# Two successive norms folded into one scale at the second mixer's entry

## The chip, the cores and the metric

One core of one Trainium2 chip runs the whole program. The time is the device time of one execution, in microseconds; of several executions the median is given. The engines are TensorE (PE, with its weight loads as PEld), VectorE (DVE), ScalarE (ACT), GpSimd (POOL) and SyncE (SP), which here issues nearly all DMAs. Each engine works its own queue in order and waits on semaphores that the others raise.

## The reference

Two transformer blocks follow one another on one sequence of 256 tokens with 1024 features, in float32. The place of the change is the seam between them: the first block ends in a norm, and the second begins with another one, with a modulation worked out from a vector `c`.

```python
def rmsnorm(x, w, eps=NORM_EPS):
    xf = x.astype(jnp.float32)
    y = xf * lax.rsqrt(jnp.mean(xf * xf, axis=-1, keepdims=True) + eps)
    return (y * w.astype(jnp.float32)).astype(x.dtype)

# first_block, end
    h = h + 0.5 * swiglu_ffn(rmsnorm(h, ffn2_norm[layer]), ffn2_w_in[layer], ffn2_w_out[layer])
    return rmsnorm(h, final_norm)

# second_block
    mod = c_act @ w_ada[l] + b_ada[l]
    shift1, scale1, gate1, shift2, scale2, gate2 = [m[:, None, :] for m in jnp.split(mod, 6, axis=-1)]
    h = rms_norm(x, g_pre_mix[l]) * (1.0 + scale1) + shift1
    y = token_mixer(h, cos, sin, w_in[l], conv_w[l], conv_b[l], ...)
    x = x + gate1 * rms_norm(y, g_post_mix[l])

# token_mixer, beginning
    z = h @ w_in
    u_glu, q_lat, kv_lat, k_r, gate_logits = jnp.split(z, IN_SPLIT, axis=-1)
    ua, ub = jnp.split(u_glu, 2, axis=-1)
    u = ua * jax.nn.sigmoid(ub)
    u = causal_depthwise_conv_2(u, conv_w, conv_b)
    u = jax.nn.silu(layer_norm(u, conv_norm_g, conv_norm_b))
```

The convolution has 31 taps on 1024 channels. The gains of the final norm are a vector, so the second norm's sum of squares is that of the first norm's output with the gains in it.

## The kernel before

Activations lie transposed, features on the 128 partitions and tokens along the row: `resid` holds eight tiles of 128 x 256. Each matrix product takes one slab of weights at a time (`PLAN` lists all 153), 128 x 2048 numbers, 256 output columns wide. A slab is loaded by SyncE into one of three slots (`raw`), ScalarE casts it to its high part (`wh`, `cast`), VectorE subtracts to get the low part (`wl`, `sub`), and TensorE makes three products for each weight tile: high by high, high by low, low by high (`wide`, line 1681). A slot's load waits for the subtraction of the slab three before, its cast for that slab's products (`taken`). The activations are split the same way into `xh` and `xl`. There is no scheduler: the order on each engine is the order in which its function is written.

The feed-forward part of the first block (`ffn`) ends with a slab whose product fills four banks; behind it VectorE adds bank after bank to the residual (line 1153, `ffn2_resid` counts 4). Then, before:

- GpSimd squares the residual pair by pair (`squares`, line 568) into `kn`, ScalarE squares it with the final norm's gain (line 874) into `qn`, and TensorE sums both over the features by products with a matrix of ones (`column_sums`, line 1709).
- VectorE multiplies the residual by the gain in place (line 1385), makes the modulation vectors `ada` and `mods` (lines 1389 to 1399), takes the first root's reciprocal `rstd` (line 1095), forms the second mean from both sums (lines 1403, 1405), waits for ScalarE's second root (line 877), takes its reciprocal, and scales tile by tile (line 1412). ScalarE adds the shift (line 880, `xh`), VectorE forms `xl` (line 1418). At the end VectorE scales the residual itself by `rstd` (line 1420).
- TensorE takes slabs glu 0 to glu 7, the first waiting tile by tile for `h_xl`. For each pair of slabs ScalarE takes a sigmoid (line 887) and VectorE multiplies (line 1442) into `upad`, the padded input of the long convolution.

The convolution is shared. GpSimd does tiles 0, 1, 6 and 7: behind the squares it clears the pads (line 603), fetches the positions by a DMA of its own (line 605), works out the rotation angles (lines 617 to 629), then multiplies and adds tap by tap (lines 641 to 648). VectorE does tiles 2 to 5 (`convolve`, lines 1430 and 1433) a few taps at a time between its other duties: subtractions, normed latents, eight attention heads. Behind the last head it waits for GpSimd (`long_conv`) and sets a marker (line 1536), on which TensorE sums the convolution over the features for the layer norm (line 2078), and VectorE subtracts the mean (`centre`, lines 1516 and 1519).

Of the kernel before, what the change touches and what calls it, by code (L numbers as in the profile page):

```python
# [11 lines left out]
ACT = mybir.ActivationFunctionType  # L12
# [46 lines left out]
for _name, _width in (("ident", P), ("ones", P), ("eps", 1), ("inv_freq", 1), ("qk_scale", 1), ("swap", P),  # L59
# [22 lines left out]
def constants():  # L82
# [46 lines left out]
    put("eps", np.full((P, 1), EPS))  # L129
    qk = np.ones((8, 1))  # L130
# [5 lines left out]
def slab_plan():  # L136
# [20 lines left out]
    for k in range(1, MLP_STEPS):  # L157
# [15 lines left out]
             ("f_stat", 2), ("lat_stat", 1), ("ln_stat", 1), ("y_stat", 1), ("x3_stat", 1), ("z_stat", 1)),  # L173
    "roots": (("n1_std", 1), ("n2_std", 1), ("qk_std", 1), ("short_std", 1), ("o_std", 1), ("n3_std", 1), ("f_std", 1),
              ("g_std", 1), ("lat_std", 2), ("ln_std", 1), ("y_std", 1), ("x3_std", 1), ("z_std", 1)),
    "inverses": (("n1_rstd", 1), ("n2_rstd", 1), ("qk_rstd", 1), ("short_rstd", 1), ("o_rstd", 1), ("n3_rstd", 1),
                 ("f_rstd", 1), ("g_rstd", 1), ("ln_rstd", 1), ("y_rstd", 1), ("x3_rstd", 1), ("z_rstd", 1)),
# [76 lines left out]
def two_blocks(nc, a):  # L254
    with ExitStack() as ctx:
# [47 lines left out]
        eps = const("eps", 1)  # L303
# [80 lines left out]
        ln_squares = tiles(w_qr, KT)  # L384
        upad_out = w_qr.rearrange("p (a n) -> p a n", a=2)
# [158 lines left out]
        def _(pool):  # L544
# [55 lines left out]
            squares("f", "ffn2_resid", kn)  # L600

            pool.wait_ge(*at("ffn2_resid", 4))
# [63 lines left out]
        def _(act):  # L666
# [38 lines left out]
            def ffn(name):  # L705
# [28 lines left out]
                if name == "ffn2":  # L734
                    cast(s0 + 3 * FF_STEPS + 2)
# [331 lines left out]
        def _(dve):  # L1067
# [33 lines left out]

            def ffn(name, n):
# [44 lines left out]
                s = s0 + 3 * FF_STEPS - 1  # L1147
                for b in range(4):
# [9 lines left out]
                if name == "ffn2":  # L1158
                    sub(s + 3)
# [219 lines left out]
            dve.wait_ge(*at("ffn2_resid", 4))  # L1379
# [787 lines left out]
```

## Time and profile before

| | before |
|---|---|
| median of 3 runs | 1180.82 us (1178.88 to 1183.17) |
| the profiled execution | 1180.76 us, span 1179.0 us |
| granted TensorE clock, mean | 0.941 |
| PE busy | 1070.3 us, 91% |
| DVE busy | 874.6 us, 74% |
| ACT busy | 471.9 us, 40% |
| POOL busy | 523.6 us, 44% |

Times inside the profile are microseconds from the first instruction of the span. An engine's row in a timeline gives the start, the length, the engine, the line, the operation with output and inputs, and in brackets how long the engine had been idle and which instruction released it. Successive instructions of one line are merged into one row with their number. A product of a float32 matrix shows as two records, so eight column sums are sixteen. The granted clock is 1.00 at the full level and 0.50 at the lower one; a value between means that it changed within the stretch. The busy shares are means over a long program with different stages and bound nothing by themselves.

### The profile page before, as it was taken

Reading aid. Unit: us, or ns where it says so; the run is one execution under the profiler, and the core shown is the slowest. Engines: PE = TensorE matmul, PEld = TensorE weight load, DVE = VectorE, ACT = ScalarE, POOL = GpSimd, SP = SyncE. Lnnn points to the kernel's source line nnn. Section 1 sums busy time; section 2 is a strip of 40 time slices with the busy share of each in tenths; the row PEclk is TensorE's granted clock in tenths of the full one; section 3 lists DMA queues with packets and bytes.
Section 4 is the critical chain, followed back from the end, with each engine's and each line's share of the span. In section 5 each row is a group of like instructions: output and inputs, shape, how many; then the busy total and the mean of one; then the engine's idle time right before and its main releaser. Section 6 shows DMA issues by size and latency. Waiting matters only on the chain.

```text
span 1179.0 us, 19793 instructions
## 1 busy us (share of the span) xinstructions
PE 1070.3 (91%) x8149; PEld 1024.1 (87%) x8149; DVE 874.6 (74%) x804; ACT 471.9 (40%) x508; POOL 523.6 (44%) x343
## 2 busy tenths in 40 slices
PE   6999999889789899999997999669779969999996
PEld 6999999787789789999997899656669959999995
DVE  4977767899578377787777689999987566555554
ACT  4433333445231344434334443443357443333331
POOL 1667667222037032466765899999940010000001
PEclk9999999898799999999999899886789989999998
DMA  9676777545430155677676264441224524555530
GB/s 320 216 239 224 249 235 234 158 123 178 122 129 0 36 163 197 213 248 237 226 249 183 75 176 118 143 125 55 72 72 132 167 95 126 190 183 178 178 106 36
DMA packets 165130, 188.81 MB, mean 160 GB/s; under 512 B 10478, under 2 KB 154428, under 8 KB 164956
## 3 DMA queue, kind: packets, MB, share of 16 engines
q1 hardware_dynamic: 164112, 185.91, 49.7%
q0 software_dynamic: 192, 1.88, 0.4%
q8 instruction: 33, 0.54, 0.2%
q10 hardware_dynamic: 780, 0.37, 0.2%
q14 instruction: 13, 0.11, 0.0%
HBM read 187.10 MB, written 1.05 MB: 160 GB/s over the span
## 4 chain that ended last, share of the span: by engine, by line
PE 68%; DVE 23%; issue 4%; ACT 3%; DMA 2%; SPq 1%; DVEq 0%; ACTq 0%
PE ps L1681 41%; PE ps L1695 17%; DVE work L1433 7%; DVE wl L1074 4%; PE ps L1831 3%; DMA raw<-in_ffn_w_in 2%; DVE work L1196 1%; ACT wh L675 1%; PE ps L1709 1%; PE ps L1815 1%; DVE rstd L1095 1%; PE ps L1807 1%; PE ps L1992 1%; DVE yl L1085 1%; PE ps L1720 1%
## 5 line engine op out<-in xcount | busy, mean ns | idle before, releaser
L1681 PE MATMUL ps<-xh,wh 128*128 128x256 f32 x1272 | 374.3, 294 | 19.1 <-DVE xl L1418 6.4
L1681 PE MATMUL ps<-xl,wh 128*128 128x256 f32 x1272 | 368.0, 289 | 0.0
L1681 PE MATMUL ps<-xh,wl 128*128 128x256 f32 x1272 | 367.7, 289 | 0.0
L1079 DVE TENSOR_TENSOR wl<-raw,wh 128x2048 fp32r<-128x2048 f32 x84 | 245.8, 2926 | 72.4 <-ACT wh L681 72.3
L1681 PEld LDWEIGHTS ps<-xh,wh 128*128 128x128 f32 x1272 | 252.3, 198 | 27.2 <-issue 18.1
L1681 PEld LDWEIGHTS ps<-xl,wh 128*128 128x128 f32 x1272 | 252.9, 199 | 0.1
L1681 PEld LDWEIGHTS ps<-xh,wl 128*128 128x128 f32 x1272 | 252.5, 198 | 0.0
L681 ACT ACTIVATE wh<-raw 128x2048 fp32r<-128x2048 f32 x84 | 160.5, 1911 | 157.1 <-PE ps L1681 157.1
L1074 DVE TENSOR_TENSOR wl<-raw,wh 128x2048 fp32r<-128x2048 f32 (+1 forms) x69 | 169.6, 2462 | 49.8 <-ACT wh L675 49.2
L554 POOL TENSOR_TENSOR ada_raw<-ada_raw,c_act 128x2048 f32<-128x2048 f32 x24 | 90.3, 3763 | 261.2 <-DMA ada_raw<-in_w_ada 244.2
L675 ACT ACTIVATE wh<-raw 128x2048 fp32r<-128x2048 f32 (+1 forms) x69 | 129.6, 1878 | 127.6 <-PE ps L1681 102.4
L1695 PE MATMUL ps<-fl,wh 128*128 128x256 f32 x560 | 157.9, 282 | 0.0
L1695 PE MATMUL ps<-fh,wl 128*128 128x256 f32 x560 | 157.8, 282 | 0.0
L1695 PE MATMUL ps<-fh,wh 128*128 128x256 f32 x560 | 157.8, 282 | 0.0
L1681 PE MATMUL ps<-yh,wh 128*128 128x256 f32 x480 | 136.9, 285 | 1.9 <-DVE yl L1570 1.3
L1681 PE MATMUL ps<-yl,wh 128*128 128x256 f32 x480 | 134.9, 281 | 0.0
L1681 PE MATMUL ps<-yh,wl 128*128 128x256 f32 x480 | 134.8, 281 | 0.0
L659 POOL TENSOR_TENSOR work<-work,rstd 128x512 f32<-128x512 f32 x2 | 3.4, 1701 | 295.1 <-DVE rstd L1095 295.1
L1695 PEld LDWEIGHTS ps<-fh,wh 128*128 128x128 f32 x560 | 105.7, 189 | 0.0
L1695 PEld LDWEIGHTS ps<-fl,wh 128*128 128x128 f32 x560 | 105.7, 189 | 0.0
L1695 PEld LDWEIGHTS ps<-fh,wl 128*128 128x128 f32 x560 | 105.6, 188 | 0.0
L644 POOL TENSOR_SCALAR ada_raw<-work,vec 128x256 f32<-128x256 f32 x120 | 101.3, 854 | 5.9
(318 smaller groups left out, 1765.2 us busy)
## 6 DMA issues: line engine op xcount, KB each, us to landing
raw<-in_ffn_w_in SPq DMA_DIRECT2D x44, 1024.0 KB, 7.4
ada_raw<-in_w_ada SPq DMA_DIRECT2D x24, 1024.0 KB, 5.4
raw<-in_ffn_w_out SPq DMA_DIRECT2D x22, 1024.0 KB, 4.9
raw<-in_w_in SPq DMA_DIRECT2D x18, 1024.0 KB, 5.4
raw<-in_w_mlp_in SPq DMA_DIRECT2D x16, 1024.0 KB, 5.6
raw<-in_w_mlp_out SPq DMA_DIRECT2D x16, 1024.0 KB, 4.9
raw<-in_w_mix_in SPq DMA_DIRECT2D x14, 1024.0 KB, 5.4
raw<-in_w_mix_out SPq DMA_DIRECT2D x4, 1024.0 KB, 4.9
```

What stands on the lines that cost most here:

```text
L554: pool.tensor_tensor(ada_raw[:, :, :], ada_raw[:, :, :], c_act[:, :].unsqueeze(2).to_broadcast([P, KT, 256]), ALU.mult).then_inc(S("ada_pa ...
L644: ins = pool.tensor_scalar(tap_mem[:, n, :], upad[:, t, k:k + T], tap(k, t), 0.0, ALU.mult, ALU.add)
L675: act.activation(wh[:, s % SLOTS, 0:n], raw[:, s % SLOTS, 0:n], ACT.Copy).then_inc(high_done, 1)
L681: act.activation(wh[:, s % SLOTS, :], raw[:, s % SLOTS, :], ACT.Copy).then_inc(high_done, 1)
L1074: dve.tensor_tensor(wl[:, s % SLOTS, 0:n], raw[:, s % SLOTS, 0:n], wh[:, s % SLOTS, 0:n].bitcast(F32), ALU.subtract).then_inc(low_done, 1)
L1079: dve.tensor_tensor(wl[:, s % SLOTS, :], raw[:, s % SLOTS, :], wh[:, s % SLOTS, :].bitcast(F32), ALU.subtract).then_inc(low_done, 1)
L1085: dve.scalar_tensor_tensor(low[:, t, :], resid[:, t, :], col(gain, t), high[:, t, :].bitcast(F32), ALU.mult, ALU.subtract).then_inc(S(n + ...
L1095: dve.reciprocal(dst, src).then_inc(S(n + "_rstd"), 1)
L1433: ins = dve.scalar_tensor_tensor(conv[:, t, :], upad[:, t, k:k + T], tap(k, t), conv[:, t, :], ALU.mult, ALU.add)
L1681: mm = pe.matmul(bank[:, m * T:(m + 1) * T], w[:, k, m * P:(m + 1) * P], r[:, k, :], start=(m == 0 and k == 0 and j == 0), stop=(k == KT - ...
L1695: mm = pe.matmul(ps[m // 2][:, (m % 2) * T:(m % 2 + 1) * T], w[:, k, m * P:(m + 1) * P], r[:, k, :], start=False, stop=False, skip_group_c ...
L1831: mm = pe.matmul(unit(bank, u % 4), lhs(u), rhs(u), start=(u % 4 == 0), stop=True, skip_group_check=True)
```

## The change

The two norms become one scale. With the sum of the squares of residual times gain coefficient as `g`, the second norm of the first norm's output is the residual over the square root of `g / D + eps squared`, where the coefficient is the root of gain squared plus eps (`final_coef`). So one column sum and one root give what two of each gave, and the product of the residual with the vectors (`mods`, now with the final gain in it) can be formed for each bank before the scale is known.

- `modulation_vectors` runs on VectorE before the residual's four additions, and behind each addition two tiles of `kn` are formed (line 1195 of the kernel after).
- ScalarE takes the small root of the coefficients, then squares; the cast of glu 2 moves behind the shifts, and so does its subtraction on VectorE.
- The scale is applied to pairs of tiles: tiles 0 to 3 on VectorE, tiles 4 to 7 on GpSimd, which waits for the scale ahead of clearing the pads.
- Slab glu 0 is multiplied input tile by input tile (`by_tile`), both halves of the output in turn.
- The first norm itself, which the residual still needs, has its column sums between glu 0 and glu 1 on TensorE, its root on ScalarE ahead of the cast of glu 3, and its reciprocal and eight scalings (`final_normed`) behind the first glu product on VectorE.

```diff
@@ gpsimd
-            squares("f", "ffn2_resid", kn)
-
-            pool.wait_ge(*at("ffn2_resid", 4))
+            squares("f", "ffn2_resid", f_squares)
+
+            pool.wait_ge(*at("h_u", 4))
+            pool.wait_ge(*at("g_rstd", 1))
+            for b in (2, 3):
+                pool.tensor_tensor(kn[:, 2 * b:2 * b + 2, :], kn[:, 2 * b:2 * b + 2, :], spread(hid[:, 0, 0:T], 2), ALU.mult)\
+                    .then_inc(S("h_f_last"), 1)
             pool.memset(upad[:, :, 0:PAD], 0.0).then_inc(S("upads"), 1)
@@ scalar, end of ffn2
-                    cast(s0 + 3 * FF_STEPS + 2)
+
+                    act.wait_ge(*at("final_sq", 1))
+                    act.activation(final_coef, final_sq, ACT.Sqrt, bias=eps).then_inc(S("final_coef"), 1)
+                    act.wait_ge(*at("final_coef", 1))
@@ scalar, entry
-                act.activation(qn[:, t, :], resid[:, t, :], ACT.Square, scale=col("final_norm", t)).then_inc(S("fg_sq"), 1)
-            root("f", ps[6][:, 0:T], std[:, :], D)
-            act.wait_ge(*at("m2", 1))
-            act.activation(kr, kr_raw, ACT.Sqrt, scale=1.0 / D, bias=eps).then_inc(S("g_std"), 1)
+                act.activation(qn[:, t, :], resid[:, t, :], ACT.Square, scale=final_coef[:, t:t + 1]).then_inc(S("fg_sq"), 1)
+
+            act.wait_ge(*at("g_stat", 1))
+            act.activation(std[:, :], ps[6][:, 0:T], ACT.Sqrt, scale=1.0 / D, bias=eps_sq).then_inc(S("g_std"), 1)
             for t in range(KT):
-                act.wait_ge(*at("h_f", t + 1))
+                act.wait_ge(*(at("h_f", t // 2 + 1) if t < 4 else at("h_f_last", t // 2 - 1)))
                 act.activation(xh[:, t, :], kn[:, t, :], ACT.Identity, bias=ada[:, t:t + 1]).then_inc(S("h_xh"), 1)
+            cast(FIRST["glu"] + 2)
+            act.wait_ge(*at("g_rstd", 1))
+            root("f", ps[1][:, 0:T], std[:, :], D)
@@ vector, end of ffn2
+                if name == "ffn2":
+                    modulation_vectors()
                 for b in range(4):
...
-                if name == "ffn2":
-                    sub(s + 3)
+                    if name == "ffn2":
+                        dve.wait_ge(*at("ffn2_resid", b + 1))
+                        for t in (2 * b, 2 * b + 1):
+                            ins = dve.tensor_scalar(kn[:, t, :], resid[:, t, :], mods[:, 0, t:t + 1], None, ALU.mult)
+                        ins.then_inc(S("h_u"), 1)
@@ vector, entry (the lines 1379 to 1412 of before go)
+            dve.wait_ge(*at("h_u", 4))
+            inverse("g", hid[:, 0, 0:T], std[:, :])
+            for b in range(2):
+                dve.tensor_tensor(kn[:, 2 * b:2 * b + 2, :], kn[:, 2 * b:2 * b + 2, :], spread(hid[:, 0, 0:T], 2), ALU.mult)\
+                    .then_inc(S("h_f"), 1)
             for t in range(KT):
                 dve.wait_ge(*at("h_xh", t + 1))
                 dve.scalar_tensor_tensor(xl[:, t, :], kn[:, t, :], ada[:, t:t + 1], xh[:, t, :].bitcast(F32), ALU.add,
                                          ALU.subtract).then_inc(S("h_xl"), 1)
-            st(dve.tensor_tensor(resid[:, :, :], resid[:, :, :], spread(rstd[:, :], KT), ALU.mult))
+            sub(FIRST["glu"] + 2)
+
+            def final_normed():
+
+                inverse("f", rstd[:, :], std[:, :])
+                for t in range(KT):
+                    dve.scalar_tensor_tensor(resid[:, t, :], resid[:, t, :], col("final_norm", t), rstd[:, :], ALU.mult, ALU.mult)
...
+                if n == 0:
+                    final_normed()
@@ tensor, wide and entry
+                order = [(m, k) for k in inputs for m in range(m_tiles)] if by_tile else \
+                    [(m, k) for m in range(m_tiles) for k in inputs]
...
-            column_sums("f", lambda k: kn[:, k, :], KT, ps[6][:, 0:T], ("f_sq", 1), by_pair=True)
-            column_sums("f", lambda k: qn[:, k, :], KT, ps[5][:, 0:T], ("fg_sq", 8))
+            for k in range(KT):
+                pe.wait_ge(*at("fg_sq", k + 1))
+                mm = pe.matmul(ps[6][:, 0:T], ones, qn[:, k, :], start=(k == 0), stop=(k == KT - 1), skip_group_check=True)
+            mm.then_inc(S("g_stat"), 1)
             for n in range(4):
...
-                wide(s, ps[4 + 2 * (n % 2)], xh, xl, "h_xl" if n == 0 else None, one)
+                wide(s, ps[4 + 2 * (n % 2)], xh, xl, "h_xl" if n == 0 else None, one, by_tile=(n == 0))
+                if n == 0:
+                    column_sums("f", lambda k: f_squares[:, k, :], KT, ps[1][:, 0:T], ("f_sq", 1), by_pair=True)
                 wide(s + 1, ps[5 + 2 * (n % 2)], xh, xl)
```

On VectorE, behind the residual's additions, before: the subtraction of glu 2, the scalings of the residual, the small vectors, and two reciprocals in a row.

```order
L1074 TENSOR_TENSOR wl<-raw,wh 128x2048
L1385 TENSOR_SCALAR resid<-resid,vec 128x256 x8
L1389 TENSOR_TENSOR ada<-ps,vec 128x48
L1396 SCALAR_TENSOR_TENSOR mods<-ada,vec 128x8
L1397 TENSOR_TENSOR mods<-ada,vec 128x8
L1398 SCALAR_TENSOR_TENSOR mods<-ada,vec 128x8
L1399 TENSOR_TENSOR mods<-ada,vec 128x8
L1095 RECIPROCAL rstd<-std 128x256
L1403 TENSOR_TENSOR work<-ps,rstd 128x256
L1405 TENSOR_TENSOR work<-work,rstd 128x256
L1095 RECIPROCAL hid<-work 128x256
L1407 TENSOR_TENSOR hid<-hid,rstd 128x256
```

On VectorE at the same place now, from the last addition on (`work` is `kn` in line 1195 and 1419, and `upad` in line 1454):

```order
L1187 SCALAR_TENSOR_TENSOR resid<-ps,resid 128x512
L1195 TENSOR_SCALAR work<-resid,mods 128x256 x2
L1108 RECIPROCAL hid<-std 128x256
L1419 TENSOR_TENSOR work<-work,hid 128x512 x2
L1423 SCALAR_TENSOR_TENSOR xl<-work,ada,xh 128x256 x8
L1087 TENSOR_TENSOR wl<-raw,wh 128x2048 x2
L1454 TENSOR_TENSOR work<-ps,hid 128x2x256
L1108 RECIPROCAL rstd<-std 128x256
L1431 SCALAR_TENSOR_TENSOR resid<-resid,vec,rstd 128x256 x8
```

One reciprocal is left ahead of the tiles; the other, with the residual's scalings, stands behind the first glu product, and glu 2's subtraction behind the tiles.

On GpSimd, from the squares to the first of the angles, before:

```order
L568 TENSOR_TENSOR work<-resid 128x512 x4
L603 MEMSET work 128x8x30
L605 DMA work<-in_positions 128x256
L617 CAST ada_raw<-work 128x256
L618 TENSOR_SCALAR ada_raw<-ada_raw,con 128x256
```

and now (line 608 is the pair of products with the scale, behind a wait for it):

```order
L571 TENSOR_TENSOR work<-resid 128x512 x4
L608 TENSOR_TENSOR work<-work,hid 128x512 x2
L610 MEMSET work 128x8x30
L612 DMA work<-in_positions 128x256
L624 CAST ada_raw<-work 128x256
```

Two products stand ahead of the pads, the positions' DMA, the angles and all taps.

## Rows read from the trace of the kernel before

**Rows 1.** Page, the chain that ended last, share of the span by line.

```profile
PE ps L1681 41%; PE ps L1695 17%; DVE work L1433 7%; DVE wl L1074 4%; PE ps L1831 3%; DMA raw<-in_ffn_w_in 2%; DVE work L1196 1%; ACT wh L675 1%; PE ps L1709 1%; PE ps L1815 1%; DVE rstd L1095 1%; PE ps L1807 1%; PE ps L1992 1%; DVE yl L1085 1%; PE ps L1720 1%
```

**Rows 2.** Timeline of VectorE at the entry: start, length, line, operation, idle before.

```profile
630.51 2.29 DVE L1079 TENSOR_TENSOR wl<-raw,wh 128x2048 fp32r<-128x2048 f32 x1 [1.11 <-ACT wh L681]
632.71 2.00 DVE L1153 SCALAR_TENSOR_TENSOR resid<-ps,resid 128x512 f32<-128x512 f32 x3
...
639.66 2.35 DVE L1385 TENSOR_SCALAR resid<-resid,vec 128x256 f32<-128x256 f32 x8
641.93 0.19 DVE L1389 TENSOR_TENSOR ada<-ps,vec 128x48 f32<-128x48 f32 x1
...
642.82 1.75 DVE L1095 RECIPROCAL rstd<-std 128x256 f32<-128x256 f32 x1
...
655.97 2.81 DVE L1420 TENSOR_TENSOR resid<-resid,rstd 128x2048 f32<-128x2048 f32 x1
```

**Rows 3.** Timeline of ScalarE at the entry and in the first slabs.

```profile
637.33 3.29 ACT L874 ACTIVATE work<-resid,vec 128x256 f32<-128x256 f32 x8
...
641.93 0.47 ACT L703 ACTIVATE std<-ps,con 128x256 f32<-128x256 f32 x1
...
660.33 1.92 ACT L675 ACTIVATE wh<-raw 128x2048 fp32r<-128x2048 f32 x1 [5.07 <-PE ps L1681]
...
671.85 1.92 ACT L675 ACTIVATE wh<-raw 128x2048 fp32r<-128x2048 f32 x1 [3.42 <-PE ps L1681]
```

**Rows 4.** Timeline of TensorE, second set of column sums and first glu product.

```profile
640.67 3.72 PE L1709 MATMUL ps<-work,con 128*128 128x256 f32 x16 [1.80 <-ACT work L874]
650.75 0.55 PE L1681 MATMUL ps<-xh,wh 128*128 128x256 f32 x1 [6.35 <-DVE xl L1418]
```

**Rows 5.** Timeline of GpSimd from the squares to its last tap.

```profile
633.48 4.04 POOL L568 TENSOR_TENSOR work<-resid 128x512 f32<-128x512 f32 x4 [9.19 <-DVE resid L1153]
637.45 0.30 POOL L603 MEMSET work<- 128x240 f32 x1
...
656.72 2.33 POOL L625 TENSOR_SCALAR work<-ada_raw 128x256 f32<-128x256 f32 x1
...
667.54 1.09 POOL L641 TENSOR_SCALAR work<-work,vec 128x256 f32<-128x256 f32 x2 [1.96 <-DVE work L1442]
...
674.07 3.21 POOL L648 TENSOR_TENSOR work<-work,ada_raw 128x512 f32<-128x512 f32 x1
...
868.02 1.33 POOL L648 TENSOR_TENSOR work<-work,ada_raw 128x512 f32<-128x512 f32 x1
```

**Rows 6.** VectorE's and TensorE's timelines and the chain (last row), end of the convolution.

```profile
868.25 3.25 DVE L1074 TENSOR_TENSOR wl<-raw,wh 128x2048 fp32r<-128x2048 f32 x1
...
872.72 0.15 DVE L1536 COPY att_col<-att_col 128x1 f32<-128x1 f32 x1
...
877.43 0.41 DVE L1516 TENSOR_SCALAR rstd<-ps 128x256 f32<-128x256 f32 x1
...
873.60 3.62 PE L2078 MATMUL ps<-work,con 128*128 128x256 f32 x16
...
880.77 3.46 PE ps L1681 x27
```

**Rows 7.** Stretches: busy time and count of PE, PEld, DVE, ACT, POOL, then granted clock, DMA share, GB/s.

```profile
646.00:648.00 2.00, 0.00 (x0) 0.00 (x0) 1.90 (x2) 0.03 (x1) 1.74 (x4) 0.72 0.00 0
...
656.00:658.00 2.00, 2.00 (x14) 2.00 (x14) 2.00 (x2) 0.00 (x0) 1.91 (x2) 0.72 0.00 0
...
958.00:959.00 1.00, 0.00 (x0) 0.00 (x0) 0.97 (x2) 0.00 (x0) 0.28 (x1) 0.50 0.00 0
```

**Rows 8.** Timeline of TensorE, eight column sums of a later norm behind a wait.

```profile
961.68 2.08 PE L1709 MATMUL ps<-work,con 128*128 128x256 f32 x4 [5.50 <-ACT work L1023]
964.08 4.64 PE L1709 MATMUL ps<-work,con 128*128 128x256 f32 x12 [0.32 <-ACT work L1023]
```

**Rows 9.** Page, DMA issues: count, size, median us to landing.

```profile
raw<-in_w_in SPq DMA_DIRECT2D x18, 1024.0 KB, 5.4
```

More of the change, by code:

```diff
@@ L58 @@
 C = {}
-for _name, _width in (("ident", P), ("ones", P), ("eps", 1), ("inv_freq", 1), ("qk_scale", 1), ("swap", P),
+for _name, _width in (("ident", P), ("ones", P), ("eps", 1), ("eps_sq", 1), ("inv_freq", 1), ("qk_scale", 1), ("swap", P),
                       ("causal", 3 * P), ("upper", P), ("levels", LEVELS * P), ("row_of", 64), ("grp_row_of", 32),
@@ L129, in constants @@
     put("eps", np.full((P, 1), EPS))
+    put("eps_sq", np.full((P, 1), EPS * EPS))
     qk = np.ones((8, 1))
@@ L384, in two_blocks @@
         ln_squares = tiles(w_qr, KT)
+        f_squares = tiles(w_qr, KT)
+        final_sq, final_coef = att_col[:, 0:KT], att_col[:, KT:2 * KT]
         upad_out = w_qr.rearrange("p (a n) -> p a n", a=2)
@@ L1100, in scaled, with modulation_vectors, vecs @@
                 return dve.tensor_tensor(dst, pair(bank[:, :]), spread(r[:, :], 2), ALU.mult)
+            def modulation_vectors():
+                def vecs(name):
+                    g, r = VECS[name]
+                    return vec[:, g * P + r:g * P + r + KT]
+                dve.tensor_tensor(final_sq, vecs("final_norm"), vecs("final_norm"), ALU.mult).then_inc(S("final_sq"), 1)
+                dve.wait_ge(*at("ada_taken", ADA_STEPS))
+                g, r = VECS["b_ada_2"]
+                st(dve.tensor_tensor(ada[:, :], ps[7][:, 0:ADA_TILES], vec[:, g * P + r:g * P + r + ADA_TILES], ALU.add))
+                st.sync()
+                st(dve.scalar_tensor_tensor(mods[:, 0, :], ada[:, 8:16], 1.0, vecs("g_pre_mix_2"), ALU.add, ALU.mult))
+                dve.tensor_tensor(mods[:, 1, :], ada[:, 16:24], vecs("g_post_mix_2"), ALU.mult)
+                dve.scalar_tensor_tensor(mods[:, 2, :], ada[:, 32:40], 1.0, vecs("g_pre_mlp_2"), ALU.add, ALU.mult)
+                dve.tensor_tensor(mods[:, 3, :], ada[:, 40:48], vecs("g_post_mlp_2"), ALU.mult)
+                st.sync()
+                st(dve.tensor_tensor(mods[:, 0, :], mods[:, 0, :], vecs("final_norm"), ALU.mult))
+                st.sync()
             def ffn(name, n):
@@ L1669, in _, with wide @@
         def _(pe):
-            def wide(s, bank, x, y, tile_ready=None, tile_base=0, slab=None, m_tiles=2, inputs=range(KT)):
+            def wide(s, bank, x, y, tile_ready=None, tile_base=0, slab=None, m_tiles=2, inputs=range(KT),
+                     by_tile=False):
                 slab = s if slab is None else slab
@@ L1675, in wide @@
                 h, l = (w[:, slab % SLOTS, 0:n].rearrange("p (k m) -> p k m", k=KT) for w in (wh, wl))
-                for m in range(m_tiles):
-                    for k in inputs:
-                        if tile_ready is not None and m == 0:
-                            pe.wait_ge(*at(tile_ready, tile_base(k)))
-                        for j, (w, r) in enumerate(((h, x), (h, y), (l, x))):
-                            mm = pe.matmul(bank[:, m * T:(m + 1) * T], w[:, k, m * P:(m + 1) * P], r[:, k, :],
-                                           start=(m == 0 and k == 0 and j == 0), stop=(k == KT - 1 and j == 2),
-                                           skip_group_check=True)
+                order = [(m, k) for k in inputs for m in range(m_tiles)] if by_tile else \
+                    [(m, k) for m in range(m_tiles) for k in inputs]
+                for m, k in order:
+                    if tile_ready is not None and m == 0:
+                        pe.wait_ge(*at(tile_ready, tile_base(k)))
+                    for j, (w, r) in enumerate(((h, x), (h, y), (l, x))):
+                        mm = pe.matmul(bank[:, m * T:(m + 1) * T], w[:, k, m * P:(m + 1) * P], r[:, k, :],
+                                       start=(m == 0 and k == 0 and j == 0), stop=(k == KT - 1 and j == 2),
+                                       skip_group_check=True)
                 if inputs[-1] == KT - 1:
```

44 lines of the change are left out of this document (5 added, 39 removed).

## The prediction

> **What bounds the kernel now.** I read the chain of work that ended last first: 58% of the span are TensorE's slab products (lines 1681 and 1695), 7% VectorE's taps of the long convolution (line 1433) and 4% slab subtractions (line 1074) [rows 1]. So there is one part where TensorE is not the bound, the convolution, and it begins right behind the place that the change rewrites. I then read the timelines of the four engines there, and last the place where the convolution's two halves meet.
>
> At the entry, VectorE adds the residual in four pieces, scales eight tiles, makes the small vectors, then runs two reciprocals with two roots between them and on ScalarE, and only then the tiles [rows 2, 3]. TensorE does the second set of column sums at 640.67 to 644.4 and waits 6.35 us for the first finished tile, at 650.75 [rows 4]. Slab glu 0 is done at 660.3, when ScalarE casts into its slot [rows 3]. From there TensorE runs a slab in 5.76 us (660.33 to 671.85 is two slabs) until VectorE's taps take over behind glu 7.
>
> GpSimd is the engine to watch. It squares the residual, clears the pads at 637.45, fetches the positions, works out the angles, and from 667.54 on does its half of the convolution without a pause until 868.02 + 1.33 = 869.35 [rows 5]. VectorE asks for that result only at 872.72, and TensorE starts the means at 873.60 [rows 6]. **GpSimd is 4.1 us early for TensorE (0.15 us goes to VectorE's marker), on a chain of 232 us.**
>
> **The change part by part.** All on the profiled execution (span 1179.0, time 1180.76, while the median is 1180.82: the same).
>
> *Residual and unscaled products.* VectorE's subtraction ends at 632.8 [rows 2]. The small vectors now come first: five instructions took 642.82 - 641.93 = 0.9; with two more and a third drain 1.2, so 634.0. Then four rounds of one residual add (2.00 for three, 0.67 each) and two tile scalings (2.35 for eight, 0.29 each) with a semaphore between: 1.3 a round alone. GpSimd squares beside it, and there an operation of its own that met VectorE took 3.21 instead of 1.33 [rows 5]; the other way round I bound a round at 2.1 and take 1.65. The last residual is there at 634.0 + 3 x 1.65 + 0.7 = 639.65, where it was at 636.1.
>
> *One sum, one root, one reciprocal.* ScalarE's squares cost 0.41 each [rows 3], TensorE adds each sum as it comes (3.72 for eight, 0.47 each, [rows 4]). Last pair squared 640.6, sum 641.1, root 0.47 [rows 3], reciprocal 1.75 [rows 2]: the scale is there at **643.4** (bounds 642.3 and 644.8 by the rounds). The root's table load now lies before the squares, beside the last down slab, at no cost.
>
> *Products on two engines.* VectorE two pairs, GpSimd two pairs, 1.04 us each on GpSimd (four squares took 4.04, the same shape, [rows 5]) and about 0.7 each on VectorE. The row of 3.21 against 1.33 shows that GpSimd stands still beside a VectorE operation with two inputs in SBUF. So GpSimd is done between 2.1 us (side by side) and 3.5 us (one after another) behind the scale; I take 2.8, 646.2. The Trainium skill (SBUF — State Buffer, "Who interferes with whom") says that such a pair is exclusive, the later one fully blocked; by that rule alone this term is 3.5 and the time 0.7 more. The rows of this trace agree with it for the subtractions.
>
> *First tile.* VectorE's two products (0.7 each, as a residual add of that shape), beside the second ScalarE's shift, then VectorE's low part (0.5 each, the shape of the root's 0.47), and semaphores between: TensorE starts at about 643.4 + 2.3 = 645.7 instead of 650.75, **5.0 earlier**.
>
> *Slab glu 0 by tile.* Its 48 products want 5.76 us at the full clock. The granted clock falls to the lower level (1.2 of 2.4 GHz) in TensorE's wait and is back at about 657.1, 6.35 us after work resumed [rows 7]. Again 6.35 us at half rate do 3.2 us of work, 2.6 remain: 654.6 instead of 660.3. The order by tile means that TensorE never waits for a tile, since six products at half rate take longer than a tile takes VectorE.
>
> *The residual's own sum.* Eight more column sums stand between glu 0 and glu 1: 3.72 us on TensorE's path, to 658.3. Net at glu 1: **2.0 us earlier**, which is what the entry brings. Its root holds ScalarE's cast of glu 3 until about 658.8; the slab is wanted two slabs later, so it is hidden. Its reciprocal and eight scalings (an eighth of line 1420's 2.81 is 0.35 [rows 2], with a start of its own I take 0.5: 1.75 + 8 x 0.5 = 5.8) stand behind the first glu product in VectorE's queue (now about 665) and push the subtraction of glu 4 to about 671 to 673.5; TensorE wants glu 4 at 658.3 + 3 x 5.76 = 675.6. Hidden by 2 us; if that cover were gone it would be late by what exceeds it. They replace one scaling of 2.81 that was hidden too [rows 2]. The subtraction of glu 2 moves from 637.5 to about 651, so SyncE's load of glu 5 is issued 12 us later; it lands in 5.4 us [rows 9] and its slot is cast only at about 670. Hidden.
>
> *GpSimd's queue.* This is the price. Behind the squares it now waits for the scale and does two products, and **everything behind them moves: pads, position DMA, angles, taps.** The pads go from 637.45 to 646.2, +8.75. The angles' end slides past the first glu product, so the wait of 1.96 at 667.54 disappears. Of VectorE's subtractions glu 2's now falls on the angles (1.9 each: 3.21 - 1.33), and since the taps now end behind VectorE's last subtraction (868.25, now about 866) that one falls on them too; the scaling of line 1420, which held one GpSimd operation for 2.33 [rows 5], is gone. Between 0 and 1.9 more, I take 1.0. End of GpSimd's half: 869.35 + 8.75 - 1.96 + 1.0 = **877.1**. Bounds: 874.5 (scale at 642.3, products side by side, nothing more) and 880.2 (scale at 644.8, one after another, a full subtraction).
>
> *What is late next.* TensorE comes to the means at 873.6 - 2.0 = 871.6 and now waits until 877.1 + 0.3 = 877.4, 5.8 us. In a wait of 5.50 us elsewhere the clock stood at the lower level; eight sums of the same shape then took from 961.68 to 968.72, less 0.32 of waiting 6.7 us [rows 7, 8], against 3.62 here [rows 6]. So the means end at 884.1 instead of 877.2. Behind them the order of work is as it was (VectorE centres at 877.43, TensorE goes on at 880.77, [rows 6]), and up to the end TensorE bounds it. Sum: **+6.9 us**, that is 1187.7.
>
> **The rivals.**
> 1. *GpSimd late, clock stays full.* Same place, sums in 3.62: 877.4 + 3.6 - 877.2 = +3.8, 1184.6. For it: the clock did not fall at once in the waits seen, in the one at 644.4 only in the slice 646 to 648. Against it: both waits shown of over 5 us ended at the lower level [rows 7, 8].
> 2. *GpSimd not last.* The entry's 2.0 us arrive whole: 1178.8. With a full clock through glu 0 (3.2 us more) 1175.6. It decides at one point: GpSimd's half must end before 871.3, that is no more than 1.9 us later than now. For it: few of GpSimd's taps would meet VectorE at first. Against it: the moved pads alone are 8.75.
> 3. *VectorE's block behind glu 0 delays a slab.* If the eight scalings take 0.8 each beside GpSimd instead of 0.5, glu 4 comes 0.5 late; that is swallowed, since GpSimd is last by 5 us. Only with further subtractions on GpSimd's path does it add, up to 1190 and more.
> 4. *The entry does not get shorter.* Slow rounds and slow products eat 2 us. The time is then still GpSimd's, near the upper bound.
>
> The other side of my forecast is rival 2.
>
> **How the numbers follow.** The least this measurement can tell from no change is about 0.3%, 3.5 us. Forecast (GpSimd last, half clock) 0.55, from 874.5 to 880.2 at GpSimd, +4.3 to +10.0. Rival 1: 0.14, +1.2 to +6.9, on both sides of the 0.3%. Rival 2: 0.19, half of it beyond 0.3%. Rivals 3 and 4: 0.12. So faster 0.10, same 0.24, slower 0.66. Range 1178.5 to 1190.8: the upper end is the forecast's, the lower takes in rival 2 without the full clock.
>
> **What would show it.** In the trace after: TensorE's first glu product about 5 us earlier; the scale's reciprocal ending near 643.4; the pads' clearing near 646; no GpSimd wait for the first glu product; a VectorE idle of some 6 us in front of the marker that follows the taps, released by GpSimd, and a lower granted clock through the means. It is wrong if VectorE's marker still follows its own taps at once, or if GpSimd ends by 871.

## The result and the profile after

| | before | after |
|---|---|---|
| median of 5 runs each | 1181.48 us (1178.88 to 1185.16) | 1189.31 us (1186.17 to 1193.29) |
| profiled execution | 1180.76 us, span 1179.0 us | 1189.31 us, span 1187.5 us |
| granted TensorE clock, mean | 0.941 | 0.935 |

The kernel after takes 1.007 times as long, 95% interval 1.0046 to 1.0094: by the ratio 8.3 us slower (the medians differ by 7.8), against the 6.9 that the sum gave. That lies inside the range.

In the profiled execution after, VectorE's subtraction ahead of the change stands at 632.30, in the one of before at 630.51 [rows 2]. No engine's work up to there is changed, and the place of this row moves by some us from one execution to the next: in the profiles of e1, e2, e5 and e6 below, which are the kernel before with an edit behind this row, it stands at 632.63, 632.95, 629.60 and 635.47. So below, a time of another kernel "set against before" has the difference of this row taken off (1.79 us for after). The differences are then those made from the entry on.

The chain that ended last, by engine and by line, from the page of after:

```profile
PE 63%; POOL 18%; DVE 10%; issue 4%; ACT 2%; DMA 2%; SPq 0%; DVEq 0%; ACTq 0%; POOLq 0%
PE ps L1697 38%; PE ps L1711 17%; POOL ada_raw L651 8%; POOL work L655 7%; PE ps L1847 3%; DMA raw<-in_ffn_w_in 2%; DVE work L1233 1%; DVE wl L1087 1%; PE ps L1725 1%; PE ps L1831 1%; PE ps L1823 1%; ACT wh L682 1%; DVE rstd L1108 1%; DVE yl L1098 1%; POOL work L648 1%
```

In [rows 1] VectorE's taps held 7% and GpSimd was not named. Now GpSimd's taps (lines 651 and 655) hold 15%: the chain runs through its half of the convolution.

VectorE's timeline at the entry (start, length, line, operation, idle before), where [rows 2] stood:

```profile
637.48 0.68 DVE L1187 SCALAR_TENSOR_TENSOR resid<-ps,resid 128x512 f32<-128x512 f32 x1
638.19 1.50 DVE L1195 TENSOR_SCALAR work<-resid,mods 128x256 f32<-128x256 f32 x2
...
644.75 1.75 DVE L1108 RECIPROCAL hid<-std 128x256 f32<-128x256 f32 x1 [0.81 <-ACT std L887]
646.53 2.36 DVE L1419 TENSOR_TENSOR work<-work,hid 128x512 f32<-128x512 f32 x2
```

VectorE's small vectors come first and end 0.5 us earlier than the prediction took. The four residual adds start at 635.33, 637.48, 639.60 and 641.73, a round of 2.13 us each, of which the two tile scalings are 1.50. The scale is there at 646.50.

GpSimd's timeline from the last square to its last tap, where [rows 5] stood:

```profile
642.49 1.04 POOL L571 TENSOR_TENSOR work<-resid 128x512 f32<-128x512 f32 x1 [1.09 <-DVE resid L1187]
646.65 3.38 POOL L608 TENSOR_TENSOR work<-work,hid 128x512 f32<-128x512 f32 x2 [3.12 <-DVE hid L1108]
649.97 0.30 POOL L610 MEMSET work<- 128x240 f32 x1
...
676.27 4.79 POOL L648 TENSOR_SCALAR work<-work,vec 128x256 f32<-128x256 f32 x2
...
878.66 1.26 POOL L655 TENSOR_TENSOR work<-work,ada_raw 128x512 f32<-128x512 f32 x1
```

TensorE's timeline at the entry, where [rows 4] stood, then VectorE's first and third glu product, to be held against 666.66 and 689.70 of before:

```profile
650.45 0.55 PE L1697 MATMUL ps<-xh,wh 128*128 128x256 f32 x1 [6.32 <-DVE xl L1423]
...
658.52 3.62 PE L1725 MATMUL ps<-work,con 128*128 128x256 f32 x16
661.79 0.47 PE L1697 MATMUL ps<-xh,wh 128*128 128x256 f32 x1
```
```profile
668.56 0.69 DVE L1454 TENSOR_TENSOR work<-ps,hid 128x512 f32<-128x512 f32 x1 [1.62 <-ACT hid L900]
...
691.61 0.69 DVE L1454 TENSOR_TENSOR work<-ps,hid 128x512 f32<-128x512 f32 x1 [1.65 <-ACT hid L900]
```

TensorE waits as long as before (6.32 against 6.35) and has its first tile at 650.45 - 1.79 = 648.66, 2.1 us earlier. Slab glu 1 starts at 660.00 set against before, where it was 660.3, and the first glu product at 666.77, where it was 666.66. Nothing of the entry is left when the first slab pair is done.

The end of the convolution, where [rows 6] stood, on VectorE and TensorE, and the granted clock there (columns as in [rows 7]):

```profile
875.40 1.01 DVE L1445 SCALAR_TENSOR_TENSOR work<-work,vec 128x256 f32<-128x256 f32 x2
880.03 0.15 DVE L1550 COPY att_col<-att_col 128x1 f32<-128x1 f32 x1 [3.62 <-POOL work L655]
...
885.68 0.42 DVE L1530 TENSOR_SCALAR rstd<-ps 128x256 f32<-128x256 f32 x1 [2.63 <-PE ps L2098]
```
```profile
880.24 5.41 PE L2098 MATMUL ps<-work,con 128*128 128x256 f32 x16 [2.89 <-DVE att_col L1550]
```
```profile
880.00:882.00 2.00, 1.76 (x6) 1.44 (x7) 1.97 (x3) 0.00 (x0) 0.00 (x0) 0.72 0.02 4
882.00:884.00 2.00, 2.00 (x6) 1.64 (x5) 1.05 (x2) 0.00 (x0) 0.00 (x0) 0.50 0.06 20
```

VectorE has done its own taps at 876.4 and stands 3.62 us before the marker, released by GpSimd. The means start at 878.45 set against before (873.60 before, +4.85), and take 5.41 instead of 3.62 since the clock falls while they run (+1.8): it is at the full level for their first 0.6 us, then at 0.50 until 884.3. VectorE subtracts the mean at 883.89 instead of 877.43, **+6.5 us**, and that distance about holds to the end of the span: 8.5 us in all, less the 1.8 that lay ahead, are 6.7.

### The profile page after: what moved, and what is told of

It reads as the page before. It is cut to its first block, busy times and chain, and to the rows that moved or that the text cites. A ratio compares the mean times of both kernels' runs of the same rounds, so it can differ in the third digit from the quotient of the medians.

```text
span 1187.5 us, 19789 instructions
## 1 busy us (share of the span) xinstructions
PE 1072.9 (90%) x8149; PEld 1025.6 (86%) x8149; DVE 890.5 (75%) x804; ACT 472.6 (40%) x509; POOL 526.5 (44%) x345
## 4 chain that ended last, share of the span: by engine, by line
PE 63%; POOL 18%; DVE 10%; issue 4%; ACT 2%; DMA 2%; SPq 0%; DVEq 0%; ACTq 0%; POOLq 0%
PE ps L1697 38%; PE ps L1711 17%; POOL ada_raw L651 8%; POOL work L655 7%; PE ps L1847 3%; DMA raw<-in_ffn_w_in 2%; DVE work L1233 1%; DVE wl L1087 1%; PE ps L1725 1%; PE ps L1831 1%; PE ps L1823 1%; ACT wh L682 1%; DVE rstd L1108 1%; DVE yl L1098 1%; POOL work L648 1%
## 5 line engine op out<-in xcount | busy, mean ns | idle before, releaser
L1092 DVE TENSOR_TENSOR wl<-raw,wh 128x2048 fp32r<-128x2048 f32 x84 | 239.1, 2846 | 61.6 <-ACT wh L688 61.6
L651 POOL TENSOR_SCALAR ada_raw<-work,vec 128x256 f32<-128x256 f32 x120 | 98.8, 834 | 5.9
```

The lines of the kernel that those rows point to most:

```text
L651: ins = pool.tensor_scalar(tap_mem[:, n, :], upad[:, t, k:k + T], tap(k, t), 0.0, ALU.mult, ALU.add)
L1092: dve.tensor_tensor(wl[:, s % SLOTS, :], raw[:, s % SLOTS, :], wh[:, s % SLOTS, :].bitcast(F32), ALU.subtract).then_inc(low_done, 1)
```

## The experiments

Twelve kernels. Each ratio is to the kernel before, measured on the same chip, with its 95% interval in brackets, and 0.001 is 1.18 us.

### Is GpSimd's end the price?

**e3** takes GpSimd's two products away (VectorE does all four), and with them its wait for the scale. ScalarE's waits for the tiles are changed to match.

```diff
@@ gpsimd, kernel after
-            pool.wait_ge(*at("h_u", 4))
-            pool.wait_ge(*at("g_rstd", 1))
-            for b in (2, 3):
...
+            pool.wait_ge(*at("ffn2_resid", 4))
@@ vector
-            for b in range(2):
+            for b in range(4):
```

> The kernel after, with all four products with the scale on VectorE; GpSimd no longer waits for the scale, only for the last residual. GpSimd theory: its pads start about 6 us earlier than in the changed kernel, its taps about 5 us earlier, its half ends within 1 to 3 us of VectorE's: 5 to 7 us less than the changed kernel, ratio to before 1.000 to 1.003. Rival, the lateness comes from the late residual and the position fetch alone: no gain over the changed kernel.

Ratio 1.0009 (0.9992 to 1.0026): 7 us of the 8.3 are gone. The products on VectorE, then the marker and the means, in its timelines:

```profile
646.17 2.90 DVE L1415 TENSOR_TENSOR work<-work,hid 128x512 f32<-128x512 f32 x4
...
876.99 0.15 DVE L1546 COPY att_col<-att_col 128x1 f32<-128x1 f32 x1 [1.24 <-POOL work L651]
```
```profile
877.20 3.72 PE L2094 MATMUL ps<-work,con 128*128 128x256 f32 x16 [0.51 <-DVE att_col L1546]
```

GpSimd is still last at the marker, by 1.24 us, but TensorE waits only 0.51 and the clock stays at the full level. Four products alone take VectorE 2.90; in the kernel after it needed 2.36 for two, beside GpSimd. Sharing them saved VectorE 0.5 us and cost the chain seven.

**e1** and **e2** set out to price GpSimd's lateness in the kernel before, with 4 products without use behind its squares in e1 (the edit below) and 10 in e2.

```diff
@@ gpsimd, kernel before, behind squares("f", ...)
+            pool.wait_ge(*at("con_rest", 16))
+            for n in range(4):
+                ps_(pool.tensor_tensor(w_v[:, 1024:1536], con[:, C["levels"]:C["levels"] + 512],
+                                       con[:, C["levels"]:C["levels"] + 512], ALU.mult))
+                ps_.sync()
```

> The kernel before, with four idle products (128 x 512, out of the constants into unused memory) on GpSimd behind its squares, about 1.12 us each: pads, angles and taps move by 4.5 us, the wait for the first glu product takes 1.96 of it, so GpSimd's half of the convolution ends near 871.9 instead of 869.35. GpSimd theory (4.1 us are free at the end): the time of before, ratio 1.000. Rival, any delay of GpSimd is paid in full: +2.5 to +4.5 us.

> The same with ten such products: GpSimd moves by 11.2 us, 9.2 behind the wait, about as far as the change moved it. The entry is that of before. GpSimd theory: its half ends near 879, VectorE idles in front of its marker, TensorE's means end 6 us later and 2 to 3 us more for the lower clock: +7 to +9 us, ratio 1.006 to 1.008. Rival, the loss of the change lies in the entry (more column sums on TensorE's path, slow rounds on VectorE): ratio 1.000.

Ratios 1.0043 (1.0023 to 1.0062) and 1.0085 (1.0056 to 1.0113). Both missed, and both for another reason. In e1 VectorE's eight scalings of line 1390, which took 2.35 alone [rows 2], lie beside these products:

```profile
641.79 5.65 DVE L1390 TENSOR_SCALAR resid<-resid,vec 128x256 f32<-128x256 f32 x8
...
879.25 0.15 DVE L1541 COPY att_col<-att_col 128x1 f32<-128x1 f32 x1
```
```profile
656.09 0.55 PE L1686 MATMUL ps<-xh,wh 128*128 128x256 f32 x1 [9.59 <-DVE xl L1423]
```

TensorE waits 9.59 for the first tile, not 6.35, and the marker follows VectorE's own taps with no idle time: GpSimd was not last; the entry came 3.9 us late. In e2 the scalings take 8.96 and the wait is 13.18; GpSimd's half ends 10.2 us later, and VectorE's own taps end later still. The two don't test the end of the convolution. They show the other direction of the conflict in [rows 5]: a GpSimd product with both inputs in SBUF holds VectorE's scalings up, though these have only one tensor input.

**e5** and **e6** delay GpSimd's taps without work beside the entry: they wait until TensorE has taken glu 2, or in e6 (with + 4 for + 3) glu 3.

```diff
@@ gpsimd, kernel before, ahead of the taps
+            pool.wait_ge(taken, FIRST["glu"] + 3)
```

> The kernel before with nothing added but a wait: GpSimd's taps begin only when TensorE has finished slab glu 2, at about 671.9 instead of 667.5, so 4.4 us later and without an instruction beside VectorE's. GpSimd theory (4.1 us free, and one subtraction of 1.9 us more may fall on its taps): 0 to +2.5 us. Rival, every delay of GpSimd is paid: +4.4.

> The same, behind slab glu 3: the taps begin at about 677.6, 10.1 us later, near where the changed kernel begins them (8.7 later). The entry is that of before. GpSimd theory: GpSimd ends near 880, VectorE idles 7 us ahead of its marker, the means run partly at the lower clock: +7 to +9 us, ratio 1.006 to 1.008. Rival, the loss lies in the entry: ratio 1.000.

Ratios 1.0023 (1.001 to 1.0037) and 1.0089 (1.0072 to 1.0106). In e5, whose subtraction ahead of the entry stands 0.91 earlier than in before, the taps start 4.6 us late:

```profile
671.23 1.09 POOL L642 TENSOR_SCALAR work<-work,vec 128x256 f32<-128x256 f32 x2 [8.63 <-PE ps L1682]
```
```profile
873.87 0.15 DVE L1537 COPY att_col<-att_col 128x1 f32<-128x1 f32 x1 [1.58 <-POOL work L649]
```
```profile
874.08 3.72 PE L2079 MATMUL ps<-work,con 128*128 128x256 f32 x16 [0.85 <-DVE att_col L1537]
```

4.6 us are just over GpSimd's 4.1 us of slack, and the whole costs 2.7 by the ratio (1.2 to 4.4), a little above the 0 to 2.5 expected. In the trace the mean's subtraction is 1.3 later. e6 at the same place:

```profile
884.34 0.15 DVE L1537 COPY att_col<-att_col 128x1 f32<-128x1 f32 x1 [3.97 <-POOL work L649]
```
```profile
884.55 6.47 PE L2079 MATMUL ps<-work,con 128*128 128x256 f32 x16 [3.24 <-DVE att_col L1537]
```

VectorE waits 3.97 us for GpSimd ahead of the marker, and TensorE 3.24 for the marker. Set against before, GpSimd's taps start 11.4 us late and its half ends 9.6 late, where the kernel after has 8.8. The cost is 10.5 us, above the 7 to 9 expected; 1.3 us of it stand already at the first glu product, where nothing is edited. These kernels have no other edit. So a later start of GpSimd's taps is enough by itself to give a loss as large as that of the kernel after.

**e9** keeps the kernel after whole and moves GpSimd's pads, position DMA and first of the two angle passes ahead of the squares, into time that GpSimd had spent waiting for the residual (9.19 in [rows 5]). Its wait for `ada_taken` goes too.

```diff
@@ gpsimd, kernel after
-            squares("f", "ffn2_resid", f_squares)
-
-            pool.wait_ge(*at("h_u", 4))
-            pool.wait_ge(*at("g_rstd", 1))
-            for b in (2, 3):
...
             pool.memset(upad[:, :, 0:PAD], 0.0).then_inc(S("upads"), 1)
...
-            pool.wait_ge(*at("ada_taken", ADA_STEPS))
...
-            for dst, quarter, shift in ((sines, 0.0, 0.0), (cosines, 0.25, float(np.float32(np.pi / 2)))):
+            def angle(dst, quarter, shift):
...
+            angle(sines, 0.0, 0.0)
+            squares("f", "ffn2_resid", f_squares)
+
+            pool.wait_ge(*at("h_u", 4))
+            pool.wait_ge(*at("g_rstd", 1))
+            for b in (2, 3):
...
+            angle(cosines, 0.25, float(np.float32(np.pi / 2)))
```

> The kernel after with one edit: GpSimd's pads, position DMA and first angle pass stand ahead of its squares of the residual, with the sums behind slab glu 0 as in the kernel after (e7 had both edits). It tells what of e7's 6.1 us gain is GpSimd's order and what the sums' place. Theory (GpSimd's late end was the loss, and the entry as I sized it for the prediction, with short rounds, is worth 2 us): GpSimd ends ahead of VectorE's own taps, the marker follows VectorE at once, no wait there, and the time is 1 to 3 us below the kernel before. The sums' place then makes up the other 3 to 5 us of e7, since the clock falls to the lower level in the wait for the scale. Rival (the order of GpSimd alone did it): within 1 us of e7, 6 us below before.

Ratio 0.9999 (0.9984 to 1.0013). All of the loss is gone: GpSimd's half ends at 867.48 set against before, and VectorE's marker follows its own taps. The entry is faster in this kernel as well, but e4 (below) shows that a faster entry by itself takes nothing off the loss, so it was GpSimd's late end. But the 1 to 3 us of gain that I expected are not there either. The entry itself brings about what the prediction had, 2.4 us at the first glu product against 2.0 at glu 1:

```profile
637.59 0.77 DVE L1196 TENSOR_SCALAR work<-resid,mods 128x256 f32<-128x256 f32 x2
...
642.67 1.75 DVE L1109 RECIPROCAL hid<-std 128x256 f32<-128x256 f32 x1 [1.52 <-ACT std L888]
...
665.45 0.69 DVE L1455 TENSOR_TENSOR work<-ps,hid 128x512 f32<-128x512 f32 x1 [1.66 <-ACT hid L901]
...
667.84 6.46 DVE L1432 SCALAR_TENSOR_TENSOR resid<-resid,vec,rstd 128x256 f32<-128x256 f32 x8
674.22 5.58 DVE L1088 TENSOR_TENSOR wl<-raw,wh 128x2048 fp32r<-128x2048 f32 x2
```

With GpSimd's squares behind the rounds, two scalings take 0.77 and a round 1.38. GpSimd's angles lie beside the rounds now; its steps with one tensor input don't stretch the scalings, and only the first round, beside a product of two tensors, took 1.87. Its subtraction ahead stands at 631.71, 1.20 later than in before, so the first glu product is at 664.25, **2.4 us earlier**. Then the residual's own norm holds VectorE (6.46 for eight scalings beside GpSimd's first taps, not 4), two slab subtractions queue behind it, and TensorE waits for one of them:

```profile
677.75 0.36 PE L1698 MATMUL ps<-xh,wh 128*128 128x256 f32 x1 [1.45 <-DVE wl L1088]
```

This is slab glu 4. The third glu product is 0.7 us ahead of before, the fourth 0.2 behind. The eight scalings take 0.8 each, the condition of rival 3, and in this trace its delay takes 1.7 of the 2.4 us by the third product; where the rest goes by the fourth is not tested.

### Can the block behind the first glu product be moved?

**e11** is e9 with the residual's norm behind the next subtraction instead of ahead of it; **e12** makes the same edit to e7 (below).

```diff
@@ vector, loop over the glu products
-                if n == 0:
-                    final_normed()
                 if n >= 2:
...
                 sub(s + 4)
+                if n == 0:
+                    final_normed()
```

> e9 (the kernel after, with GpSimd's pads, position DMA and first angle pass ahead of its squares) with one edit: the residual's own norm (reciprocal and eight scalings, final_normed) stands on VectorE behind the subtraction that follows the first glu product, not ahead of it. In e9 the first glu product came 2.4 us earlier than before, and TensorE then waited 2.1 us for slab subtractions of VectorE (1.45 at the longest); the second glu product was 0.3 later than before. Theory (that queue of the residual's norm ahead of the subtraction took back the entry's gain): the wait of 1.45 goes, the second glu product comes 1.5 to 2 us earlier than in e9, and the ratio to the kernel before falls from 1.000 to about 0.9985, 1 to 2 us. Rival (VectorE's own work sets the end of the convolution, and the eight scalings cost it the same wherever they stand): the second glu product comes earlier, but the marker does not, and the time is that of e9 within 0.7 us.

> e7 (the fastest so far: GpSimd's first angle pass ahead of its squares, and the residual's column sums in TensorE's wait for the scale) with the same edit as e11: the residual's norm behind the subtraction that follows the first glu product. TensorE waited 1.0 us for slab subtractions there in e7. Theory: 0.5 to 1 us below e7, a ratio of about 0.995 to the kernel before. Rival as in e11: equal to e7 within 0.5 us.

e11: 0.9984 (0.9967 to 1.0002). Its third glu product:

```profile
688.70 0.69 DVE L1455 TENSOR_TENSOR work<-ps,hid 128x512 f32<-128x512 f32 x1 [2.00 <-ACT hid L901]
```

Less 1.37, the distance ahead, it is at 687.33, and 2.4 us ahead of before: TensorE's wait for glu 4 is gone and the gain kept up to there. The second glu product, which I expected 1.5 to 2 us earlier than in e9, is 0.4 later (680.34, 678.97 set against before), since the scalings now stand right ahead of it on VectorE. At the mean's subtraction 1.3 us are left. By the ratios e9 and e11 can't be told apart (their intervals overlap), so that the time gains by this edit is not shown; only the wait is shown to go. e12: 0.9949 (0.993 to 0.9969), where e7 has 0.9955, the same within its interval. There the rival held: the third glu product is 0.6 us earlier than in e7, the marker not (866.32 against 866.37 set against before).

### What the sums' place is worth

**e4** moves the residual's column sums from behind slab glu 0 into TensorE's wait for the scale; **e7** does so in e9.

```diff
@@ tensor, entry
             mm.then_inc(S("g_stat"), 1)
+            column_sums("f", lambda k: f_squares[:, k, :], KT, ps[1][:, 0:T], ("f_sq", 1), by_pair=True)
...
-                if n == 0:
-                    column_sums("f", lambda k: f_squares[:, k, :], KT, ps[1][:, 0:T], ("f_sq", 1), by_pair=True)
```

> The kernel after, with the eight column sums of the residual's own norm moved from behind glu 0 into TensorE's wait for the scale ahead of it. Entry: glu 1 starts 3.7 us earlier, more if the clock falls later. GpSimd theory: the end of the convolution is GpSimd's, so the time stays that of the changed kernel within 1 us (GpSimd's taps start no earlier). Rival, the sums on TensorE's path are the loss: 3.7 us less than the changed kernel.

> The kernel after with two moves. On GpSimd the pads, the positions' DMA and the first half of the angles stand ahead of the squares, in its wait of 10 us for the residual; on TensorE the column sums of the residual's own norm stand in the wait for the scale. GpSimd still does two of the four products. GpSimd theory: its taps begin with the first glu product, which comes some 5 us earlier than in the kernel before, and VectorE's marker follows its own taps: 4 to 6 us less than before, ratio 0.995 to 0.9965. Rival, the squares that now come later hold up TensorE or VectorE: ratio 0.998 or more.

e4: 1.0066 (1.0043 to 1.009), as slow as the kernel after, though its first tiles came in another way. TensorE's entry and VectorE's marker in e4:

```profile
650.05 0.35 PE L1697 MATMUL ps<-xh,wh 128*128 128x256 f32 x1 [2.86 <-DVE xl L1423]
```
```profile
879.23 0.15 DVE L1550 COPY att_col<-att_col 128x1 f32<-128x1 f32 x1 [8.36 <-POOL work L655]
```

The first glu product is at 662.47, with its subtraction ahead at 631.91: set against before, 5.7 us earlier than in after. 3.6 are the sums; the rest, 2.1, goes with the clock, which stays at the full level from the wait on (0.35 for the first product, 0.55 in after). Most of this turns into idle time before the marker, 8.36 instead of 3.62, and the rest is lost on the way. A gain on TensorE and VectorE is worth nothing while GpSimd is last.

e7, with GpSimd no longer last: 1175.96 against 1182.10 us, 0.9955 (0.9937 to 0.9973). **It beats both kernels.** The first glu product is at 660.32, 6.6 us earlier set against before, and at the marker VectorE follows its own taps:

```profile
867.98 0.15 DVE L1551 COPY att_col<-att_col 128x1 f32<-128x1 f32 x1
```

**e8** is e7 with all four products on VectorE.

> The same, with all four products with the scale on VectorE. Two products shared took VectorE 2.36 us, four alone 2.90, so VectorE loses 0.5 us and GpSimd is free 3 us earlier, where it has nothing to gain any more. Theory: the time of the kernel with shared products within 1 us. Rival, shared products keep VectorE and GpSimd from each other further on: 2 us less.

0.9968 (0.9954 to 0.9982), a median of 1178.43 us against e7's 1175.96. The two intervals overlap, so a difference is not shown; but 2.5 us lie between the medians where I expected less than 1, and that is not shown either. In the traces the mean's subtraction is 0.8 later than in e7. The rival, 2 us less than e7, is out.

### The order by tile

**e10** multiplies slab glu 0 half by half, as before.

```diff
-                wide(s, ps[4 + 2 * (n % 2)], xh, xl, "h_xl" if n == 0 else None, one, by_tile=(n == 0))
+                wide(s, ps[4 + 2 * (n % 2)], xh, xl, "h_xl" if n == 0 else None, one)
```

> The kernel after with slab glu 0 multiplied half by half of its output as before, instead of input tile by input tile. My sum gave the order by tile no price, since three products at half rate take longer than a tile takes VectorE (0.7 against 0.5). Theory: within 1 us of the kernel after. Rival (the order by tile saves waits of the first half): TensorE waits for tiles between the products of the first half, glu 0 ends later, but GpSimd is last at the marker all the same and the time stays; then the first glu product comes 1 us or more later in the trace and the time is within 1 us too.

1.0063 (1.0039 to 1.0088), as the kernel after. Its first wait is 6.31, there is no further one in the slab, and the first glu product is at the same place (669.39 with its subtraction ahead at 633.14). The order by tile neither costs nor brings anything here.

## Why the prediction was right, and where its terms were not

The verdict, its sign and its mechanism held: GpSimd's chain decides, at the place that was named, and the experiments e3, e5, e6 and e9 show it. That the sum came within 1.4 us of the measured time is in part luck, since terms were off both ways. Term by term, all set against before:

- **Rounds.** Taken at 1.65, bounds 1.3 and 2.1; measured 2.13. GpSimd's square of 1.04 stretches two scalings from 0.77 (e9) to 1.50. That is the upper bound plus a little; with the small vectors 0.5 shorter than taken, the last residual came at 640.6 instead of 639.65 and the scale at 644.7 instead of 643.4, just inside its bound of 644.8. It is the first term that was mis-sized.
- **Products on two engines.** Taken at 2.8 behind the scale, between 2.1 and 3.5; the two took 3.38 and ended 3.5 behind it. The row of 3.21 against 1.33 was the better guide. By the rule of the Trainium skill ("SBUF — State Buffer", "Who interferes with whom") the term is 3.5. The trace agrees with it here, 3.5 measured. GpSimd's two products end at 648.2 instead of 646.2.
- **First tile.** Taken at 2.3 behind the scale, 645.7; measured 3.95 behind it, 648.66. Of the 2.3, 1.4 were VectorE's two products and 0.9 what follows. The products took 2.36, in turns with GpSimd's, and 1.6 pass from the start of the low parts (648.82) to the first product. Here the term missed most, by 1.65 besides the late scale.
- **Slab glu 0.** 8.9 us were taken, 8.07 came: the clock returned 5.1 us after work resumed, not 6.35. The slab was done at 656.7 instead of 654.6. Entry at glu 1: 0.3 us earlier instead of 2.0, and 0 at the first glu product. Rival 4, with a chance inside the 0.12, came true beside the forecast. It too left the time to GpSimd, and then the entry changes nothing: e4 gave the entry 5.7 us and the time stayed.
- **Residual's own norm.** Eight scalings took 4.81, 0.6 each (0.5 taken). TensorE did not wait for glu 4: the glu products follow at 11.52 us, as before, so the cover was enough. Rival 3 did not come up in this kernel; e9, where the scalings take 0.8 and the entry is shorter, shows a wait of 1.45 by it.
- **GpSimd.** The pads moved by 10.73 instead of 8.75, and the wait of 1.96 went. 869.35 + 10.73 - 1.96 = 878.12, and the half ends at 879.92 - 1.79 = 878.13. So the 1.0 for meetings with subtractions was nothing in sum: from the pads to the first tap GpSimd took 26.3 us instead of 28.1 without the wait, and the taps took 1.8 more. The scale 1.3 later, the products 0.7 longer and the meetings 1.0 less put the half's end 1.0 later than forecast, inside its bounds of 874.5 (the prediction's own terms give 874.3) and 880.2.
- **The means.** TensorE was to come at 871.6 and wait 5.8; it came at 875.6 and waited 2.89. The entry's 2.0 were lost, and 2.0 more came behind it, which the prediction did not have: the fourth glu product is 1.1 late, behind slab subtractions that take 5.75 us where they took 4.66, and TensorE's first product with the normed latents, for which it waits on VectorE (749.67, 746.25 before), 1.6. The clock fell while the sums ran: 5.41 instead of the 6.7 taken, 3.62 at the full level. The centre was forecast at 884.1 + 0.2 and came at 883.89.

The last points make the sum: 1.0 later at GpSimd, 1.3 less in the means, +6.5 in the trace against the +6.9 of the sum. Two errors cancelled in part. Rival 1's mechanism, a clock that stays full, came true in half. Rival 2 was to decide at 871.3: GpSimd's end was 6.8 us past it. Its worth, 1178.8 from the entry's 2.0 us, is not borne out either, for e9 puts GpSimd ahead of that point, with 2.4 us at the first glu product, and gets 0.9999 (0.9984 to 1.0013). In the chances rival 1's 0.14 stands wholly under same, though its sum, +3.8, lies past the 3.5 us that the prediction sets as the limit.

What stays open: the ratio says 8.3 us (5.4 to 11.1), the trace 6.5 from the entry on. The other 1.8 lie ahead of the change in one pair of executions. The row that they are read from stands between 629.6 and 635.5 in the five profiles of kernels made from before and between 629.9 and 633.1 in the nine made from after, so the traces give no ground to put them down to the change.

## What to carry to other kernels

Before giving a waiting engine a piece of the critical path, read how much slack its own chain has at the place where it is next asked for: here 4.1 us over 232, and the work and its wait moved that chain by 8.8. If its queue holds work that needs nothing from the critical path, put that ahead of the wait; this alone took the loss to nothing (e9), and with the sums in TensorE's idle time it made a gain (e7). A gain at the entry has to be followed to the next queue: in e9's trace one block of VectorE work behind the first product took 1.7 of its 2.4 us.

## What the runs showed of the hardware

- A GpSimd operation with two inputs in SBUF holds up VectorE's scalings of one tensor by a column: two of 128x256 take 1.50 us beside a square of 1.04, and 0.75 to 0.79 beside GpSimd steps with one tensor input (e9); eight take 5.65 beside four products and 8.96 beside ten, 2.35 alone.
- Products of 128x512 on both engines at once take turns: VectorE's two take 2.36 us and GpSimd's two 3.38; four on VectorE alone take 2.90.
- The clock does not need a long wait to fall, and it can fall behind it: after waits of 0.51 and 0.85 the eight sums took 3.72, after 2.89 they took 5.41, with the full level for the first 0.6 us and 0.50 behind; after 3.24 (e6) 6.47, after 7.63 (e4) 5.86. The wait for the first tile, cut from 6.32 to 2.86 by sums inside it (e4), left the first product at the full level.
- GpSimd's taps are not of a fixed length: from the first to the last they took 201.8 us in before, 203.6 in after and 197.9 in e4. But from the clearing of the pads to the last tap, with the angles and less the wait of 1.96, it was 229.9, 230.0 and 229.6 us. In these three kernels the time of the pads was enough to tell when GpSimd's half ends.
